# Mixer output projection in two halves with the row factor at the addition, and new borders between stages

## The chip, the cores and the metric

One core of one Trainium2 chip runs the kernel. The metric is the device time of one execution in microseconds (us), the median over several runs. Engines are called PE (TensorE), DVE (VectorE), ACT (ScalarE), POOL (GpSimd) and SP (SyncE, which issues the DMAs). SBUF is the on-chip memory, PSUM the accumulation memory of eight banks that PE writes.

## What is computed

256 tokens of width 1024 go through three layers. Layer 0 is causal attention (16 heads of 64) with q, k rotated and normalized, gated by silu(z), then an output product and a gated addition ("PLE": `x + sigmoid(norm(x) @ w_gate) * (p @ w_proj)`). Layer 1 is a three-branch attention with the same frame. Layer 2 is a mixer (half recurrent, half chunk attention), an attention over 256 memory rows, and an expert layer. The mixer's end is what the title speaks of:

```python
y = concat([rmsnorm(lru_half, norm_grp_a), rmsnorm(attended_half, norm_grp_b)])
x = x + y @ w_out            # rmsnorm(v, g) = v * rsqrt(mean(v * v) + eps) * g, per token
x = x + memory_attention(rmsnorm(x, norm_cross), rmsnorm(mem, norm_mem), ...)
```

A row factor of `rmsnorm` is one number per token, so it can be applied after the product with `w_out`; the gain `g` is per channel and can't.

## The kernel before, in words

**Products in three parts.** All dense products are done in a split form: each fp32 matrix is a high part (`whi`, `hThi`, type fp32r) and a remainder (`wlo`, `hTlo`). A product is the sum of `whi*hThi`, `wlo*hThi` and `whi*hTlo`. Weights come in 88 units of 1 MB (128 x 2048), two units (halves) per chunk of 512 columns. A unit takes 48 matmuls of 256 columns: 16 for each of the three parts. SP loads units into a ring of four slots (L542). ACT writes `whi` (`split`, L1251), of which there are two, so the split of unit u waits for PE's end of unit u-2. POOL writes `wlo = slot - whi` (L1183). PE waits on `hi_ready` and `lo_ready`.

**Activations.** The input of a product is x, transposed on PE by a product with the identity into PSUM, as four "pieces" of 256 channels (`piece`, L641), and then split by ACT or DVE (`piece_hi_act` L1287, `piece_hi_dve` L1782, `piece_lo_dve` L1793). Both wait until PE has ended the last unit that reads the old activations:

```python
def piece_hi_act(name, u):
    act.wait_ge(piece_done, pieces_before(name) + u + 1)
    act.wait_ge(proj_done, units_before(name))
```

The first unit with new activations is `unit_of_pieces` (L663): high parts of pieces 0 and 1, the transposes of the last piece (`last_piece`), high parts of pieces 2 and 3, then all of `wlo`, then the low parts. Chunks in `UNITWISE` go by tokens (`unit_by_tokens`, L691), the others through `project` (L733, L736). The very first activations, `norm0`, have a path of their own: transposes of x (L632), a product with the gain (L1712), a cast (L1716), and remainders on POOL and DVE (L1721). It starts once x, `keep` (the identity) and all of `sml` (gains, tables, p transposed) have landed.

**Row factors.** ACT sums squares (`squares`, L1236), DVE computes mean plus eps (`rsqrt`, L1667), ACT takes the root (L1230), DVE takes the reciprocal and one Newton step (L1669 to L1673), each waiting for the one before. `row_scale` copies the result for ACT (L1694, L1695). All these small operands lie in SBUF (`sc8`). `inverse_root` (L1725 to L1732) does the like for q and k in `rope_chunk`. The constants of the recurrence (`lam`, L1978 on) are computed after the first `row_scale`, in a ping-pong of DVE and ACT (L1367, L1369).

**The stages in question.** After the mixer's inputs (`mix_in`, five chunks), the row scales of the recurrent half go through `rsqrt`, `diagonals` on ACT (L1433) and `row_of_scales` on PE (L953). Then PE waits until ACT has taken v out of PSUM (L1276), and `attention(2)` runs 16 jobs (8 heads x 2 token tiles), software-pipelined: PE scores (L836), DVE maximum (L1876), ACT exponential (L1357), PE transpose (L843), ACT copy (L1348), PE product with v (L854), DVE normalization per group of four jobs (L1887). Then `by_halves` (L994) does the first chunk of `w_out`. Its first half of channels comes from the recurrence (`hThi[:, 0:4]`), its second from the attention, which must first be normalized (`row_norm`, L1685), transposed (`heads`, L1001), multiplied with the gain (L2149) and split (L2153), one token tile after the other. Both weight units are held until the end. A second chunk follows, with the memory rows' pieces transposed in its middle (`memory`). Then come the chunks `mem_k`, `mem_v`, `mem_q`, `attention(3)` (8 jobs), `mem_o` (L663 on), four query chunks, and from about 770 us on the expert layer, which is not touched. The order on every engine is written out by hand.

## Time and profile before

| | us |
|---|---|
| median of 3 runs (lowest to highest) | 1599.39 (1599.07 to 1599.74) |
| the profiled execution, its own time | 1597.65 |
| its span, first to last instruction | 1595.8 |
| PE busy, of the span | 1522.0 |
| DVE, ACT, POOL busy | 897.4, 829.7, 541.1 |
| granted TensorE clock, mean | 0.989 |

PE is busy in 95% of the span, so what matters is where it is not, and what it waited for there. Outside of the start and the end, its idle time comes in many stretches of 0.3 to 4.3 us, between 119 and 732 us. The row "PEclk" of the page gives the granted clock in 40 slices; it is below full in only a few.

### The profile page before, as it was taken

How to read it: one execution, taken by the hardware profiler on the slowest of the kernel's cores; microseconds unless marked ns; L12 is line 12 of the kernel's file. 1: busy time of each engine (PE TensorE's matmuls, PEld its weight loads, DVE VectorE, ACT ScalarE, POOL GpSimd, SP SyncE). 2: the span in 40 equal slices, each digit the busy share in tenths (PEclk: the TensorE clock that was granted, in tenths of full speed). 3: DMA queues.
4: the chain of work that ended last, by engine and by line, in shares of the span. 5: the costliest groups of instructions: out<-in, count | busy, mean ns of one | idle time of the engine just before them, and what ended most of it. 6: DMA issues, size and time to landing. Idle time of an engine off the chain costs nothing.

```text
span 1595.8 us, 27986 instructions
## 1 busy us (share of the span) xinstructions
PE 1522.0 (95%) x10651; PEld 1405.9 (88%) x10651; DVE 897.4 (56%) x2088; ACT 829.7 (52%) x1502; POOL 541.1 (34%) x188
## 2 busy tenths in 40 slices
PE   5999999999999889898999999999999999999998
PEld 5998899978889789888999889999999999999886
DVE  6835348478345532132896995555555555555555
ACT  4546444478355544444455994444444444444444
POOL 5771656510356537726588980000000000000000
PEclk9999999999999899999999999999999999999999
DMA  6741334510134414434254015555555555555553
GB/s 262 285 162 52 127 137 159 211 54 2 55 131 149 168 59 165 148 110 147 80 197 155 1 53 186 186 184 185 184 187 185 188 185 187 186 187 186 173 188 131
DMA packets 37532, 238.51 MB, mean 149 GB/s; under 512 B 4160, under 2 KB 4288, under 8 KB 13248
## 3 DMA queue, kind: packets, MB, share of 16 engines
q1 hardware_dynamic: 37440, 237.27, 42.2%
q8 instruction: 59, 0.97, 0.2%
q14 instruction: 33, 0.27, 0.1%
HBM read 236.21 MB, written 1.05 MB: 149 GB/s over the span
## 4 chain that ended last, share of the span: by engine, by line
PE 67%; ACT 4%; DVE 3%; POOL 3%; issue 2%; ACTq 0%; DVEq 0%
PE bank L1128 22%; PE bank L648 15%; PE bank L651 8%; PE bank L733 5%; PE bank L736 3%; POOL wlo L1183 3%; PE bank L836 3%; PE bank L854 2%; PE bank L691 2%; PE bank L1108 2%; PE bank L663 2%; ACT whi L1251 1%; PE bank L843 1%; PE bank L641 1%; ACT arena L1561 1%
## 5 line engine op out<-in xcount | busy, mean ns | idle before, releaser
L1183 POOL TENSOR_TENSOR wlo<-raw,whi 128x2048 fp32r<-128x2048 f32 x42 | 193.8, 4615 | 199.9 <-ACT whi L1251 199.9
L1183 POOL TENSOR_TENSOR wlo<-arena,whi 128x2048 fp32r<-128x2048 f32 x42 | 194.6, 4638 | 182.9 <-ACT whi L1251 182.9
L648 PE MATMUL bank<-hThi,whi 128*128 128x256 f32 x1024 | 250.3, 282 | 0.0
L648 PE MATMUL bank<-hTlo,whi 128*128 128x256 f32 x1024 | 250.1, 282 | 0.0
L1128 PE MATMUL bank<-whi,ghi 128*128 128x512 f32 x512 | 203.1, 397 | 0.5 <-DVE glo L2307 0.5
L1128 PE MATMUL bank<-whi,glo 128*128 128x512 f32 x512 | 202.9, 396 | 0.0
L1128 PE MATMUL bank<-wlo,ghi 128*128 128x512 f32 x512 | 202.1, 395 | 0.0
L648 PEld LDWEIGHTS bank<-hTlo,whi 128*128 128x128 f32 x1024 | 195.0, 190 | 4.2 <-issue 0.2
L648 PEld LDWEIGHTS bank<-hThi,whi 128*128 128x128 f32 x1024 | 194.7, 190 | 4.2 <-issue 0.2
L1587 ACT ACTIVATE gact<-bank 128x256 f32<-128x256 f32 x96 | 37.1, 386 | 260.5 <-PE bank L651 260.5
L2302 DVE TENSOR_TENSOR gact<-gact,arena 128x256 f32<-128x256 f32 x96 | 40.8, 425 | 189.8 <-ACT gact L1587 189.8
L651 PE MATMUL bank<-hThi,wlo 128*128 128x256 f32 x1024 | 143.7, 283 | 0.0
L1251 ACT ACTIVATE whi<-raw 128x2048 fp32r<-128x2048 f32 x42 | 80.4, 1915 | 105.3 <-PE bank L736 60.4
L651 PEld LDWEIGHTS bank<-hThi,wlo 128*128 128x128 f32 x1024 | 132.1, 192 | 0.0
L1251 ACT ACTIVATE whi<-arena 128x2048 fp32r<-128x2048 f32 x42 | 80.4, 1914 | 99.4 <-PE bank L736 46.2
L2297 DVE TENSOR_TENSOR wlo<-raw,whi 128x1024 fp32r<-128x1024 f32 x84 | 102.9, 1225 | 36.8 <-ACT whi L1591 36.8
L1128 PEld LDWEIGHTS bank<-whi,glo 128*128 128x128 f32 x512 | 96.6, 189 | 23.2
L1128 PEld LDWEIGHTS bank<-whi,ghi 128*128 128x128 f32 x512 | 96.6, 189 | 20.3 <-DVE wlo L2297 1.5
L1128 PEld LDWEIGHTS bank<-wlo,ghi 128*128 128x128 f32 x512 | 96.7, 189 | 19.4
L736 PE MATMUL bank<-whi,hThi 128*128 128x256 f32 x672 | 90.1, 287 | 5.2 <-DVE hThi L1716 5.0
L836 PE MATMUL bank<-arena 128*128 128x256 f32 (+1 forms) x320 | 87.2, 365 | 6.2 <-ACT arena L1276 5.3
L736 PE MATMUL bank<-wlo,hThi 128*128 128x256 f32 x672 | 87.7, 283 | 2.6 <-POOL wlo L1183 2.5
(338 smaller groups left out, 3159.3 us busy)
## 6 DMA issues: line engine op xcount, KB each, us to landing
raw<-ex_in SPq DMA_DIRECT2D x64, 1024.0 KB, 4.7
raw<-w_in SPq DMA_DIRECT2D x44, 1024.0 KB, 4.8
arena<-w_in SPq DMA_DIRECT2D x44, 1024.0 KB, 4.7
xw<-ex_in SPq DMA_DIRECT2D x32, 1024.0 KB, 4.7
raw<-ex_in SPq DMA_DIRECT2D x54, 512.0 KB, 4.1
xw<-ex_in SPq DMA_DIRECT2D x10, 512.0 KB, 4.3
arena<-frt_in SPq DMA_DIRECT2D x1, 3904.0 KB, 15.0
arena<-tab_in SPq DMA_DIRECT2D x1, 1089.0 KB, 16.6
```

The lines of the kernel that those rows point to most:

```text
L648: mm(out, lhs, rhs, start=(k == 0), stop=False)
L651: last = mm(out, lhs, rhs, start=False, stop=(k == len(lo_pairs) - 1))
L663: last = mm(bank[2 * (c % 2) + j][:, 0:UC], lhs, rhs, start=first and k == 0, stop=final and k == KT - 1)
L733: last = mm(bank[2 * (c % 2) + b][:, T * at:T * at + T], w[:, k, P * j:P * j + P], h[:, k, :], start=first, stop=final)
L736: last = mm(bank[2 * (c % 2) + j][:, UC * half:UC * half + UC], h[:, k, P * j:P * j + P], w[:, k, :], start=first, stop=final)
L836: last = mm(score_bank(phase, i)[:, 0:j["nk"]], j["q"][k], j["k"][k], start=(k == 0), stop=(k == len(j["q"]) - 1))
L1128: last = mm(bank[2 * t + h][:, :], g[:, j % 2, tok], w[:, b, at], start=False, stop=(final and i == 2), skip_group_check=True)
L1183: G.tensor_tensor(wlo[:, u % 2, :], slots[u % RING], whi[:, u % 2, :], ALU.subtract).then_inc(lo_ready, 1)
L1251: A(whi[:, u % 2, :], slots[u % RING], ACT.Copy).then_inc(hi_ready, 1)
L1587: A(gact[:, i % 2, :], bank[4 + i % 2][:, 0:T], ACT.Gelu_apprx_tanh).then_inc(a_gelu, 1)
L2297: V.tensor_tensor(wlo[:, b, at], xslots[ex_slot(i)][:, D:2 * D], whi[:, b, at], ALU.subtract).then_inc(vlo_ready, 1)
L2302: V.tensor_tensor(gact[:, i % 2, :], gact[:, i % 2, :], weights, ALU.mult).then_inc(g_ready, 1)
```

## The change

In the parts that matter:

1. **Mixer output.** `by_halves` becomes `by_parts`: unit by unit, each token tile's two halves of channels go to two halves of a bank. The attended half is transposed without its row factor, the first token tile inside `attention(2)` (`heads(0)`), the second after the first 12 matmuls of the projection. `add_parts` adds the first half, then the second times `x_scale`. The second chunk goes the same way.
2. **First rows.** `norm0` becomes pieces like the others. SP issues `keep`, x in two token tiles, the 72 columns of gains, the four weight units, and only then the rest of `sml`. The first two units take `wlo` last. The `lam` constants are computed between the rope chunks.
3. **Borders.** High parts of new activations wait for `hThi_free`, which PE signals after its last read of `hThi`, not at the unit's end. `unit_of_pieces` does three pieces (two for `mem_o`) with their `wlo` before `last_piece`. `unit_by_tokens` takes `wlo` last in its first half. In `take_ple` piece 1 comes before the last tanh.
4. **Small operands in PSUM.** `rsqrt` and `inverse_root` keep theirs in unused columns of a bank.
5. **Around the attentions.** PE's wait for ACT's take of v moves to job 4. One split moves from the last take of `mem_q` into `attention(3)`, and the exponential's table is loaded before it.

```diff
@@ first loads
-            sp_.dma_start(x, x_d).then_inc(x_loaded, 16)
-            sp_.dma_start(keep[:, :], keep_d).then_inc(tab_loaded, 16)
-            sp_.dma_start(sml, sml_d).then_inc(tab_loaded, 16)
+            sp_.dma_start(keep[:, :], keep_d).then_inc(keep_loaded, 16)
+            for t in range(TT):
+                sp_.dma_start(x[:, t], x_d[:, t]).then_inc(x_loaded[t], 16)
+            sp_.dma_start(sml[:, 0:n_gains], sml_d[:, 0:n_gains]).then_inc(gains_loaded, 16)
...
             for u in range(RING):
                 load(u)
+            sp_.dma_start(sml[:, n_gains:NSML], sml_d[:, n_gains:NSML]).then_inc(sml_loaded, 16)
@@ unit_of_pieces
-                for u in range(4):
-                    pe.wait_ge(piece_hi[u], nth(name))
-                    pair(wh, hThi, (2 * u, 2 * u + 1), first=True)
-                    if u == 1 and last_piece is not None:
+                early = 2 if name == "mem_o" else 4 if last_piece is None else 3
...
+                for us in (range(early), range(early, 4)):
+                    if us and us[0] > 0:
                         last_piece()
-                pe.wait_ge(lo_ready, split_before(2 * c) + 1)
-                pair(wl, hThi, range(KT))
+                    for u in us:
+                        pe.wait_ge(piece_hi[u], nth(name))
+                        pair(wh, hThi, (2 * u, 2 * u + 1), first=True)
+                    if c > 0 and us:
+                        pe.wait_ge(lo_ready, split_before(2 * c) + 1)
+                        pair(wl, hThi, range(2 * us[0], 2 * us[-1] + 2))
@@ unit_by_tokens
-                pe.wait_ge(lo_ready, split_before(u) + 1)
...
+                    parts = ((wh, hThi), (wl, hThi), (wh, hTlo)) if half == 1 else ((wh, hThi), (wh, hTlo), (wl, hThi))
+                    for i, (w, h) in enumerate(parts):
+                        if w is wl and j == 0:
+                            pe.wait_ge(lo_ready, split_before(u) + 1)
...
+                        if u in LAST_READS and (i, j) == (1, 1):
+                            last.then_inc(hThi_free, 1)
@@ piece_hi_act (piece_hi_dve alike)
-                act.wait_ge(proj_done, units_before(name))
+                if units_before(name) > 0:
+                    act.wait_ge(hThi_free, frees_before(name))
@@ attention(2) and (3)
+                    if phase == 2 and i == 4:
+                        pe.wait_ge(takenA, taken_before(first_of("mix_out"), "A"))
+                    if phase == 2 and i == 14:
+                        pe.wait_ge(yn_ready, 1)
+                        pe.wait_ge(o_taken, PHASES[2][7]["number"] + 1)
+                        heads(0)
...
-                    if phase == 2 and i == 5:
+                    if (phase, i) in ((2, 5), (3, 1)):
                         split()
@@ the projection on PE
+            def by_parts(i, between):
+                c = first_of("mix_out") + i
+                for half in range(2):
...
+                    late = (i, half) == (1, 0)
+                    def part(j, side):
+                        parts = ((wh, hThi), (wh, hTlo), (wl, hThi)) if late else ((wh, hThi), (wl, hThi), (wh, hTlo))
...
+                    if (i, half) == (0, 0):
+                        part(0, 0)
+                        pe.wait_ge(o_taken, PHASES[2][-1]["number"] + 1)
+                        heads(1)
+                        part(1, 0)
+                        part(0, 1)
+                        pe.wait_ge(half_lo, 2)
+                        part(1, 1).then_inc(proj_done, 1)
+                        continue
@@ rsqrt
-                V.tensor_scalar(var[:, 0:n], of[:, 0:n], inv, EPS, ALU.mult, ALU.add).then_inc(var_ready, 1)
+                v, z = small(count[1], n)
+                y = tmp[:, 0:n]
+                V.tensor_scalar(v, of[:, 0:n], inv, EPS, ALU.mult, ALU.add).then_inc(var_ready, 1)
                 dve.wait_ge(root_ready, count[1])
-                step(V.reciprocal(rinv[:, 0:n], root[:, 0:n]))
-                step(V.tensor_tensor(tmp[:, 0:n], rinv[:, 0:n], rinv[:, 0:n], ALU.mult))
...
+                step(V.reciprocal(y, root[:, 0:n]))
+                step(V.tensor_tensor(z, v, y, ALU.mult))
...
@@ after attention(2) on DVE
-            attended = OR[:, :, CW:D]
-            row_norm(attended, attended, 512, 1, half_rows)
...
+            heads_hi(1)
+            heads_lo(1)
+            squared[0] += 1
+            dve.wait_ge(ss_ready, squared[0])
+            dve.wait_ge(half_lo, 2)
+            y, z = rsqrt(2, 1.0 / 512)
+            step(V.tensor_tensor(x_scale, z, y, ALU.mult))
             row_norm(MEM, MEM, D, 1, piece_rows)
+            add_parts(0, 0)
+            add_parts(0, 1)
+            add_parts(1, 0)
             piece_hi_dve("mem", 1)
             piece_hi_dve("mem", 3)
-            add_chunk(c + 1, 1)
             rest_of_pieces("mem")
+            add_parts(1, 1)
```

PE's instructions at the first chunk of `w_out` before, from the last low part of the recurrent half on (L1001 are the transposes of the attended half, `keep` holds the identity):

```order
L994 MATMUL bank<-whi,hTlo 128x256 x4
L1001 MATMUL bank<-keep,arena 128x128 [waits half_rows]
L1001 MATMUL bank<-keep,arena 128x128 x3
L994 MATMUL bank<-whi,hThi 128x256 [waits half_lo,half_hi]
L994 MATMUL bank<-whi,hThi 128x256 x3
L994 MATMUL bank<-wlo,hThi 128x256 x4
L994 MATMUL bank<-whi,hTlo 128x256 x4
L1001 MATMUL bank<-keep,arena 128x128 [waits half_rows]
L1001 MATMUL bank<-keep,arena 128x128 x3
L994 MATMUL bank<-whi,hThi 128x256 [waits half_lo,half_hi]
```

And now, from the projection's first matmul on (L837 are the transposes, those of the first token tile being already behind):

```order
L1030 MATMUL bank<-whi,hTlo 128x256 x4
L837 MATMUL bank<-keep,arena 128x128 [waits o_taken]
L837 MATMUL bank<-keep,arena 128x128 x3
L1030 MATMUL bank<-whi,hThi 128x256 x4
L1030 MATMUL bank<-wlo,hThi 128x256 x4
L1030 MATMUL bank<-whi,hTlo 128x256 x4
L1030 MATMUL bank<-whi,hThi 128x256 x4
L1030 MATMUL bank<-wlo,hThi 128x256 x4
L1030 MATMUL bank<-whi,hTlo 128x256 x4
L1030 MATMUL bank<-whi,hThi 128x256 [waits half_lo]
```

Where two round trips to DVE stood directly behind the transposes, 24 matmuls now stand between the only transposes left and the wait for them.

ACT's first instructions before (L1236 are the sums of squares, L1251 the splits of weights, L1367 and L1369 the steps of `lam`):

```order
L1236 ACTIVATE arena,sc<-xw 128x1024 [waits x_loaded]
L1236 ACTIVATE arena,sc<-xw 128x1024 [waits achain]
L1251 ACTIVATE whi<-raw 128x2048 [waits w_loaded0]
L1251 ACTIVATE whi<-raw 128x2048 [waits w_loaded1]
L1230 ACT_TABLE_LOAD
L1230 ACTIVATE sc<-sc 128x2 [waits var_ready]
L1367 ACT_TABLE_LOAD
L1367 ACTIVATE arena<-arena 128x4 [waits lam_v]
L1369 ACT_TABLE_LOAD
L1369 ACTIVATE arena<-arena 128x4 [waits lam_v]
L1251 ACTIVATE whi<-arena 128x2048 [waits proj_done,w_loaded2,scale_ready]
```

And now (L1388 and L1395 are the sums of squares, L1312 the high parts of pieces, L1275 the splits):

```order
L1388 ACTIVATE arena,sc<-xw 128x1024 [waits x_loaded0]
L1312 ACTIVATE hThi<-bank,arena 128x256 [waits piece_done,gains_loaded,achain]
L1312 ACTIVATE hThi<-bank,arena 128x256
L1312 ACTIVATE hThi<-bank,arena 128x256 [waits piece_done]
L1312 ACTIVATE hThi<-bank,arena 128x256
L1275 ACTIVATE whi<-raw 128x2048 [waits w_loaded0]
L1275 ACTIVATE whi<-raw 128x2048 [waits w_loaded1]
L1395 ACTIVATE arena,sc<-xw 128x1024 [waits x_loaded1]
L1254 ACT_TABLE_LOAD
L1254 ACTIVATE sc<-bank 128x2 [waits var_ready]
L1275 ACTIVATE whi<-arena 128x2048 [waits proj_done,w_loaded2,scale_ready]
```

The two steps of `lam` no longer stand ahead of the third split, and two pieces of the activations stand ahead of the first.

## Rows read from the trace of the kernel before

**Rows 1.** The page: busy time, share and instructions of each engine.
```profile
PE 1522.0 (95%) x10651; PEld 1405.9 (88%) x10651; DVE 897.4 (56%) x2088; ACT 829.7 (52%) x1502; POOL 541.1 (34%) x188
```

**Rows 2.** Who PE waited for, whole span: us in total, times, longest us.
```profile
PE bank L733 <- POOL wlo L1183: 5.3, 7, 2.0
...
PE bank L663 <- ACT hThi L1287: 4.3, 4, 1.1
...
PE bank L691 <- POOL wlo L1183: 3.2, 3, 1.1
```

**Rows 3.** Timeline, 0 to 60 us: start, duration, engine, operation, count [idle <-releaser].
```profile
8.72 4.10 PE L632 MATMUL bank<-keep,xw 128*128 128x128 f32 x16 [8.72 <-DVEq L1974]
...
11.04 1.91 ACT L1251 ACTIVATE whi<-raw 128x2048 fp32r<-128x2048 f32 x1 [2.93 <-DMA raw<-w_in]
...
13.03 4.50 POOL L1183 TENSOR_TENSOR wlo<-raw,whi 128x2048 fp32r<-128x2048 f32 x1 [12.58 <-ACT whi L1251]
...
13.52 1.91 ACT L1251 ACTIVATE whi<-raw 128x2048 fp32r<-128x2048 f32 x1 [0.57 <-DMA raw<-w_in]
13.75 4.07 DVE L1716 CAST hThi<-arena 128x512 fp32r<-128x512 f32 x1
...
17.88 3.42 PE L736 MATMUL bank<-whi,hThi 128*128 128x256 f32 x16 [5.05 <-DVE hThi L1716]
...
21.14 2.08 PE L736 MATMUL bank<-wlo,hThi 128*128 128x256 f32 x16
...
35.73 2.18 PE L736 MATMUL bank<-wlo,hThi 128*128 128x256 f32 x16 [2.48 <-POOL wlo L1183]
...
39.67 2.08 PE L736 MATMUL bank<-whi,hThi 128*128 128x256 f32 x16
```

**Rows 4.** DMA issues, 0 to 60 us: median us to landing.
```profile
arena<-sml_in SPq DMA_DIRECT2D x1, 772.0 KB, 6.9
```

**Rows 5.** Timeline, 150 to 223 us: first unit of the first PLE gate.
```profile
180.61 1.19 PE L663 MATMUL bank<-whi,hThi 128*128 128x256 f32 x8 [1.08 <-ACT hThi L1287]
...
187.42 2.08 PE L736 MATMUL bank<-whi,hThi 128*128 128x256 f32 x16
```

**Rows 6.** Timeline, 466 to 514 us: row scale of the mixer input, and what waits.
```profile
477.67 2.48 DVE L1667 TENSOR_SCALAR sc<-sc 128x2 f32<-128x2 f32 x1 [0.17 <-ACT arena L1236]
...
482.28 1.90 ACT L1251 ACTIVATE whi<-raw 128x2048 fp32r<-128x2048 f32 x1
...
488.88 1.22 PE L733 MATMUL bank<-hThi,wlo 128*128 128x256 f32 x8 [1.98 <-POOL wlo L1183]
```

**Rows 7.** Timeline, 514 to 558 us: start of the mixer's attention.
```profile
535.97 4.37 DVE L1670 TENSOR_TENSOR sc<-sc 128x2 f32<-128x2 f32 x1
...
540.37 0.16 DVE L1671 TENSOR_TENSOR sc<-sc 128x2 f32<-128x2 f32 x1
...
541.86 0.68 PE L953 MATMUL bank<-arena 128*128 128x128 f32 x4 [0.70 <-ACT arena L1433]
...
545.30 0.40 ACT L1357 ACTIVATE arena<-arena,sc 128x128 f32<-128x128 f32 x1 [0.91 <-DVE sc L1876]
```

**Rows 8.** Windows: stretch, length, busy of PE, PEld, DVE, ACT, POOL; clock, DMA share, GB/s.
```profile
546.00:556.00 10.00, 8.82 (x33) 7.05 (x33) 4.54 (x21) 7.91 (x27) 4.53 (x1) 0.52 0.09 16
```

**Rows 9.** Timeline, 557 to 620 us: the mixer's output projection.
```profile
564.83 0.72 PE L994 MATMUL bank<-whi,hThi 128*128 128x256 f32 x4
...
573.31 0.89 PE L994 MATMUL bank<-whi,hThi 128*128 128x256 f32 x4 [2.04 <-DVE hTlo L2153]
...
583.19 2.08 PE L736 MATMUL bank<-whi,hThi 128*128 128x256 f32 x16
...
598.02 2.15 PE L663 MATMUL bank<-hThi,whi 128*128 128x256 f32 x16 [1.08 <-ACT hThi L1287]
```

**Rows 10.** Timeline, 637 to 682 us: start of the memory attention.
```profile
675.97 5.41 PE L836 MATMUL bank<-arena 128*128 128x256 f32 x16 [2.54 <-ACT arena L1276]
...
678.49 0.51 ACT L1357 ACTIVATE arena<-arena,sc 128x256 f32<-128x256 f32 x1 [1.26 <-DVE sc L1876]
```

305 lines of the change are left out of this document (165 added, 140 removed).

## The prediction

> **What bounds the kernel now.** I read the page first, then the waits of PE, then the timeline at each place that the change touches. The page shows PE busy for 1522.0 of 1595.8 us [rows 1], so at most 74 us can be won, and only where PE stands idle or runs at a lower clock. The waits [rows 2] name the releasers: ACT's high parts L1287 at the first unit after a change of activations (four waits, 4.3 in all), POOL's `wlo` in `unit_by_tokens` (three, 3.2) and in `project` (seven, 5.3). The rest lies at the start, where the first matmul begins at 17.88 [rows 3], and around the mixer's attention [rows 7 to 9]. From 770 us on nothing is changed and the time only shifts.
>
> **The unit of account.** A group of 16 matmuls costs 1.92: its record says 2.08, but records overlap by 0.16 (17.88 + 3.42 is 0.16 past the next start, 21.14) [rows 3]. A weight unit is three groups, 5.76. ACT's split takes 1.91, POOL's `wlo` 4.50 [rows 3].
>
> **1. Start: 9.9 (7.5 to 10.5).** The first 17.88 us hold three things in sequence: x, `keep` and 772 KB of `sml` landing 6.9 after issue [rows 4], 4.10 of transposes from 8.72, and casts on DVE. The last cast takes 4.07, exactly beside POOL's first `wlo` [rows 3]. Now only 36 KB of gains go ahead of the weights, so 736 KB fewer. Two weight units of 1024 KB let ACT's splits begin 2.48 apart (11.04 and 13.52) [rows 3], so 736 KB are worth 1.8: first split at 9.2, first weights high at 11.15, first `wlo` at 15.7. The activations come earlier and no cast stands beside POOL. First matmul at 11.2. The first group is slow again (3.26 from start to start), the low parts follow to 16.4, then `wlo`: the first unit ends at 18.3, the second at 24.05. The third split must wait for the end of the first unit: 18.3 + 1.91 + 4.6 makes its `wlo` ready at 24.8, while PE wants it at 26.0. So the wait of 2.48 at 35.73 goes too, since no step of `lam` stands ahead of that split any more. The fourth unit starts at 29.8 instead of 39.67. The low end keeps the 2.4.
>
> **2. `unit_by_tokens`, `wlo` last in the first half: 3.2 (1.6 to 3.2).** Three waits of 1.07 [rows 2]; in that half 16 matmuls of low parts (1.92) come before `wlo` is needed, more than each wait. What is late next is the following split, which the low end pays.
>
> **3. First units with three pieces ahead: 1.15 (-0.5 to 2.2).** The high parts may start when PE has made its last read of `hThi`, one group of eight (0.96) before the unit's end, so most of the 1.08 in front of the first matmul goes [rows 5]. In exchange the last piece's transposes stand later, with one pair behind them: the way through DVE, which took 2.04 with low parts [rows 9], is without them about 1.0 and mostly bare, of which I take 0.5 as new. Net 0.55 for each of two PLE units, 0.25 and 0.2 for two others, 0.2 for `mem_o`, and -0.6 for the layer 1 output, where more stands bare. The low end is all six with the 1.0 bare and half of the gain.
>
> **4. Row scale of the mixer input: 1.8 (0.7 to 2.5).** DVE's operation on 2 elements at 477.67 takes 2.48, until POOL's `wlo` is over; the same kind takes 0.16 elsewhere [rows 6, 7]. The split at 482.28 stands behind it, and PE waits 1.98 at 488.88 for its `wlo`. With the operand in PSUM, 2.3 of ACT's delay go and the wait ends in part on the next link. The Trainium skill ("SBUF — State Buffer", "Who interferes with whom") says that DVE and GpSimd share a port pair which the one that holds it keeps for a whole instruction. The trace agrees (2.48 and 4.37 where 0.16 is usual). By that page the steps of `lam`, which stay in SBUF and now stand between the rope chunks, can each be blocked as well.
>
> **5. Start of the mixer's attention: 3.95 (2.4 to 5.4).** The same block costs 4.37 at 535.97 where 0.16 stands at 540.37 [rows 7]. ACT's diagonals, PE's four matmuls at 541.86 and the take of v follow it, and the first exponential comes at 545.30. Unblocked, the scale is ready 4.2 earlier, before PE ends `mix_in` at 541.16; ACT takes v at once, and PE's scores no longer wait for it. First exponential 542.45: 2.85. From 546 to 556 the granted clock is 0.52, so PE is nearly all the time at 1.2 GHz, after this idle; PE is busy 8.82 of 10 there and ACT 7.91 [rows 8]. At 2.4 GHz ACT would bound it, so at most 2.1 come back; I take 1.5, and 0.4 off for the first tile's transposes inside.
>
> **6. Mixer output: 5.8 (3.5 to 7).** Before, from 564.83 to the ready end of the second chunk, 598.02 - 1.08 = 596.94, are 32.1 [rows 9]. The new order needs four units (23.04), four transposes (0.48) and the memory's 16 (1.67): 25.2. The two waits of 2.04 and the slow matmuls behind the first (0.89 for four, elsewhere 0.72 or less) go, since 24 matmuls (2.9) stand ahead of the wait for the second tile, whose way through DVE took 2.04. New is a wait in the second chunk: its first split needs PE to be done with the first unit and ACT to be through its roots and squares, which I estimate at 7.2 after the attention's end from the durations of these operations, so with 1.9 and 4.6 `wlo` stands at 13.8 where PE wants it at 12.65: 1.2. That gives 26.4, a gain of 5.7, and 0.1 at the memory's pieces: their high parts start earlier, but DVE's additions come in front.
>
> **7. Cross border: 1.4 (0.5 to 1.6).** One more wait of 1.08 by the same row [rows 2], whole here since `hThi_free` comes 1.92 before the end, and 0.3 of waits for `wlo` behind it.
>
> **8. Memory attention: 2.0 (0 to 3).** PE waits 2.54 for ACT's take, behind a split of 1.91; the first exponential is at 678.49 [rows 10]. Without the split ahead it comes about 3 earlier, and 1 is given back where the split now stands between two jobs.
>
> **9. `lam` between the rope chunks: -0.5 (-3.6 to 0).** The steps have all operands in SBUF, and one caught beside POOL may last 4.4 [rows 7]. ACT waits for them within its takes. PE has a unit's cover, so I take little; the low end is one block of 4.4 with 0.8 hidden.
>
> The sum is 28.7 (all low ends 12.1, all high ends 35.4). The profiled execution has 1597.65, so 1569.0; the median is 1.74 above it: **1570.7**.
>
> **The rivals.** **A, the chain hands the waits back (0.15).** Nothing speeds up ACT or POOL; each split waits for PE's end two units before, and POOL adds 4.5. Where a wait for `wlo` goes, the next unit may meet the chain one step later, as the seven waits in `project` show [rows 2]. Against it: a split and a `wlo` are 6.4 against two units of 11.5, so a delay dies out within a unit if ACT is free. It would cost term 2 whole (3.2), 1.0 of term 4, 0.5 of term 7 and 3.6 of terms 6 and 8: 20.4 are left, 1579.
>
> **C, at the mixer output the change doesn't do what it says (0.10).** DVE has the last group's normalization, the first tile's split and both parts of the second tile in sequence; if PE's last part waits there as before, 4.5 of term 6 are lost: 1575.2.
>
> **B, slower (0.03).** TensorE stays at its lower level after the new start. The first matmuls run at half speed before: 3.26 for the first group, 1.92 for the second [rows 3]. The new start has transposes, idle, and one group after another with waits for low parts and `wlo`. Each unit at 1.2 GHz adds 5.76; the gain of 28.7 and the 3.2 that count as no change are gone after 5.5 units, and the time is over 1602.6. Against it: PE did rise within one group before, after 5.05 of idle. The Trainium skill ("TensorE: Matmul & The Clock Gate", "What's actually happening") says that the slow level is the default and activity lifts it; the trace agrees, and 10 us at 0.52 in the attention show that broken work can keep it low [rows 8].
>
> **How the numbers follow.** My forecast has 0.70, A 0.15, C 0.10, B 0.03, and 0.02 are for smaller losses that together leave no change. A measurement of this kernel can tell 0.2%, 3.2 us, from no change. Faster is then 0.95, same 0.02, slower 0.03. The range: independent errors of the terms (the largest 2.4 on terms 1 and 6) give some 5 to either side, 1564 to 1576; case A and its mixtures reach to 1583.
>
> **What would show it.** In the new profile: first matmul near 11, fourth unit near 29.8; no wait of L691's kind; every operation of `rsqrt` at 0.16 to 0.2; the first exponential of the mixer's attention 2.9 sooner after `mix_in`, and a granted clock near 1 there; no wait of 2.04 in the output, one of about 1.2 in its second chunk; about 1.0 of idle behind the last piece. Wrong would be: waits for `wlo` in the units after those named, DVE late with the second tile, or a low clock over whole units behind 11 us.

## The result and the profile after

| | before | changed |
|---|---|---|
| median of 4 executions, us | 1599.23 | 1570.53 |
| lowest to highest | 1597.09 to 1599.74 | 1569.33 to 1571.22 |
| profiled execution, its own time | 1597.65 | 1571.22 |
| its span | 1595.8 | 1569.4 |

The ratio is 0.9825, 95% interval 0.9813 to 0.9838. The forecast was 1570.7, so the time is right. The two profiled executions lie 26.4 apart, though, not 28.7: the sum of the terms was taken from the own time of the profiled one (1597.65 to 1569.0), and against that pair it was some 2.2 too high. That the medians agree to 0.2 is in part luck. Which terms held is read from the traces. One execution of a kernel below (u3, 1970.65) had a granted clock of 0.69 over its whole span and is left out of that kernel's median.

The page of the changed kernel, its busy times; they answer to [rows 1]:

```profile
PE 1513.6 (96%) x10651; PEld 1401.3 (89%) x10651; DVE 872.7 (56%) x2097; ACT 830.7 (53%) x1507; POOL 538.0 (34%) x186
```

Who PE waited for in the changed kernel (us in total, times, longest us), against [rows 2]:

```profile
PE bank L749 <- POOL wlo L1206: 4.6, 6, 1.7
PE bank L650 <- DVE arena L2260: 4.3, 1, 4.3
PE bank L673 <- DVE hThi L1813: 3.9, 5, 0.8
PE bank L673 <- DVE hThi L1811: 3.1, 3, 1.6
PE bank L673 <- ACT whi L1275: 2.7, 1, 2.7
...
PE bank L673 <- ACT hThi L1312: 1.6, 3, 0.6
...
PE bank L1030 <- POOL wlo L1206: 1.1, 1, 1.1
```

The three waits of `unit_by_tokens` are gone. The wait of 4.3 before the last border, for the scaled rows, was there before. The waits for ACT's high parts have gone from 4.3 to 1.6, and in their place stand waits for the last piece's high parts from DVE: 3.9 and 3.1, of which one of 1.57 is the last heads' in `mem_o`, as before.

The timeline of the changed kernel, 0 to 60 us (start, duration, engine, operation, count, idle and releaser), against [rows 3]:

```profile
5.53 3.64 PE L650 MATMUL bank<-keep,xw 128*128 128x128 f32 x16 [5.53 <-DMA xw<-x_in]
...
9.88 1.93 ACT L1275 ACTIVATE whi<-raw 128x2048 fp32r<-128x2048 f32 x1
...
11.86 3.78 PE L673 MATMUL bank<-whi,hThi 128*128 128x256 f32 x16 [2.69 <-ACT whi L1275]
11.89 9.13 POOL L1206 TENSOR_TENSOR wlo<-raw,whi 128x2048 fp32r<-128x2048 f32 x2 [11.43 <-ACT whi L1275]
...
15.45 3.09 PE L673 MATMUL bank<-whi,hTlo 128*128 128x256 f32 x16
...
18.37 2.08 PE L673 MATMUL bank<-wlo,hThi 128*128 128x256 f32 x16
...
31.81 2.08 PE L752 MATMUL bank<-whi,hThi 128*128 128x256 f32 x16
...
51.74 4.27 DVE L2065 TENSOR_TENSOR arena<-arena,sc 128x4 f32<-128x4 f32 x1
```

From the first start to the second are 3.59, to the third 2.92: both groups are slow, and the fourth unit starts at 31.81 where it started at 39.67. No wait is left inside. The last row is a step of `lam`, held up beside a `wlo` of POOL (51.35 to 55.98) as term 9 feared, 4.27 long; PE's groups went on 1.92 apart behind it, so it cost nothing.

The mixer's attention in the changed kernel, 512 to 546 us, against [rows 7]:

```profile
521.49 0.17 DVE L1707 TENSOR_TENSOR bank<-bank,sc 128x2 f32<-128x2 f32 x1
...
527.69 0.40 ACT L1383 ACTIVATE arena<-arena,sc 128x128 f32<-128x128 f32 x1
...
530.37 1.89 ACT L1275 ACTIVATE whi<-raw 128x2048 fp32r<-128x2048 f32 x1
...
532.48 0.43 PE L878 MATMUL bank<-arena 128*128 128x64 f32 x2 [1.94 <-ACT arena L1374]
```

And the windows there (stretch, length, busy of PE, PEld, DVE, ACT, POOL, granted clock, DMA share, GB/s), against [rows 8]:

```profile
530.00:535.00 5.00, 2.40 (x14) 1.83 (x14) 1.14 (x8) 4.84 (x13) 2.66 (x1) 0.82 0.02 5
535.00:540.00 5.00, 5.00 (x18) 3.94 (x17) 2.59 (x9) 2.61 (x9) 1.87 (x1) 0.50 0.39 138
```

The operation on two elements takes 0.17 where it took 4.37, and the first exponential comes at once. But from 535 to 540 PE is at 1.2 GHz, busy all of the time: the lower clock has come back, behind the 1.94 in which PE waited while ACT did a split.

The output projection of the changed kernel, 540 to 600 us, against [rows 9]:

```profile
548.02 0.72 PE L1030 MATMUL bank<-whi,hThi 128*128 128x256 f32 x4
...
562.27 0.74 PE L1030 MATMUL bank<-wlo,hThi 128*128 128x256 f32 x4 [1.11 <-POOL wlo L1206]
...
590.26 1.22 PE L749 MATMUL bank<-hThi,wlo 128*128 128x256 f32 x8 [1.66 <-POOL wlo L1206]
```

Neither wait of 2.04 is left, and one of 1.11 for `wlo` has come: forecast was 1.2. The wait at 590.26, behind the first unit on the memory rows, was 1.14 before (at 612.34) and is now 0.52 longer.

### The profile page after: what moved, and what is told of

The parts are those of the page before. It is cut to its first block, busy times and chain, and to the rows that moved or that the text cites. A ratio compares the mean times of both kernels' runs of the same rounds, so it can differ in the third digit from the quotient of the medians.

```text
span 1569.4 us, 28028 instructions
## 1 busy us (share of the span) xinstructions
PE 1513.6 (96%) x10651; PEld 1401.3 (89%) x10651; DVE 872.7 (56%) x2097; ACT 830.7 (53%) x1507; POOL 538.0 (34%) x186
## 4 chain that ended last, share of the span: by engine, by line
PE 52%; ACT 2%; issue 1%; DVE 1%; POOL 1%; DMA 0%; ACTq 0%; DVEq 0%
PE bank L1158 22%; PE bank L658 15%; PE bank L661 8%; PE bank L749 2%; PE bank L1138 2%; PE bank L673 1%; ACT arena L1595 1%; POOL wlo L1206 1%; ACT xw L1598 1%; PE bank L1097 0%; PE bank L752 0%; PE bank L709 0%; DMA raw<-ex_in 0%; DVE wlo L2367 0%; ACT raw L1605 0%
## 5 line engine op out<-in xcount | busy, mean ns | idle before, releaser
L1275 ACT ACTIVATE whi<-arena 128x2048 fp32r<-128x2048 f32 x42 | 80.4, 1915 | 102.9 <-PE bank L752 47.7
L1275 ACT ACTIVATE whi<-raw 128x2048 fp32r<-128x2048 f32 x42 | 80.4, 1914 | 94.1 <-PE bank L752 52.9
L1625 ACT ACTIVATE whi<-raw 128x1024 fp32r<-128x1024 f32 x84 | 88.4, 1053 | 2.1 <-DMA raw<-ex_in 2.1
L860 PE MATMUL bank<-arena 128*128 128x256 f32 (+1 forms) x320 | 84.0, 354 | 2.4 <-ACT arena L1300 1.6
L1940 DVE CUSTOM_DVE_ANT_0 arena<-bank,arena 128x256 f32<-128x256 f32 (+1 forms) x152 | 51.9, 344 | 61.8 <-PE bank L860 42.8
```

What stands on the lines that cost most here:

```text
L860: last = mm(score_bank(phase, i)[:, 0:j["nk"]], j["q"][k], j["k"][k], start=(k == 0), stop=(k == len(j["q"]) - 1))
L1275: A(whi[:, u % 2, :], slots[u % RING], ACT.Copy).then_inc(hi_ready, 1)
L1625: A(whi[:, b, at], xslots[ex_slot(i)][:, D:2 * D], ACT.Copy).then_inc(vhi_ready, 1)
L1940: V.tensor_tensor_reduce(out=Msb[n % 3][:, 0:j["nk"]], in0=score_bank(phase, i)[:, 0:j["nk"]], in1=j["mask"], scale=-j["scale"], scalar=1e ...
```

## Where the time came from, term by term

ACT's 84 splits come in the same order in both kernels, so the difference of their starts tells how far the changed one is ahead. It stands still within the long runs of units, and steps at the borders. In us:

| place (terms of the sum) | ahead behind it | step | forecast |
|---|---|---|---|
| start (1) | 7.86 | 7.9 | 9.9 |
| first eight chunks, layer 0 attention (9) | 7.8 | 0.0 | -0.5 |
| first PLE, one `unit_by_tokens` (2, 3) | 10.0 | 2.1 | 2.1 |
| layer 1 attention and first output unit (3) | 11.6 | 1.6 | -0.6 |
| second PLE, one `unit_by_tokens` (2, 3) | 13.3 | 1.8 | 1.6 |
| mixer input (4) | 14.7 | 1.3 | 1.8 |
| mixer's attention (5) | 16.8 | 2.15 | 3.95 |
| mixer output (6) | 22.1 | 5.25 | 5.8 |
| cross border (7) | 23.5 | 1.5 | 1.4 |
| memory attention and `mem_o` (8, 3) | 26.5 | 2.95 | 2.2 |
| last `unit_by_tokens` and last border (2) | 26.5 | 0.1 | 1.1 |

(For the mixer's attention the first matmul of the projection is compared, 564.83 and 548.02.) Three terms were too large by 2.0, 1.8 and 1.0, two too small by 2.2 and 0.7. The experiments are about these.

## Experiments: one part undone

Each kernel is the changed one with the edit that is shown, and is compared with the changed one's 1570.53. The groups of experiments ran at other times and on other chips than it. Between the groups the median of the kernel before lay between 1598.2 and 1599.3, so a difference of about one microsecond from 1570.53 tells nothing. One execution of each kernel has a trace. "Split by split" compares the starts of ACT's 84 splits in two traces, as in the table.

All four ran beside the kernel before on the same chip (1598.83, 7 executions).

**The small operands back in SBUF (u1).**

```diff
-            b = bank[small_bank[call - 1]]
-            return [b[:, 464 + 16 * i:464 + 16 * i + n] for i in range(2)]
+            return [var[:, 8 * i:8 * i + n] for i in range(2)]
```

> The changed kernel with one thing undone: the two small operands of rsqrt lie in SBUF again, not in PSUM. My theory (DVE is held up by POOL wherever an operation has all operands in SBUF): an operation of rsqrt that meets a wlo of POOL lasts 2 to 4.4 us again, and the two places lose what they won: about 1.3 at the mixer input (where the trace of the change won that much between the splits), 2.9 at the first exponential of the mixer's attention; together some 4 us, 1574.5, with 0.5 more or less elsewhere. Rival (the earlier first exponential comes from PE's scores no longer waiting for the take): rsqrt may be held up, but the attention starts as in the change, and at most 1.5 are lost, 1572.

Measured: 1575.06, ratio to the kernel before 0.9847 (0.9831 to 0.9864). Its timeline at the start of the mixer's attention:

```profile
524.89 4.37 DVE L1705 TENSOR_TENSOR sc<-sc 128x2 f32<-128x2 f32 x1
...
533.20 0.40 ACT L1382 ACTIVATE arena<-arena,sc 128x128 f32<-128x128 f32 x1
```

and at the mixer input:

```profile
468.33 0.72 DVE L1702 TENSOR_SCALAR sc<-sc 128x2 f32<-128x2 f32 x1
...
477.80 1.21 PE L748 MATMUL bank<-hThi,wlo 128*128 128x256 f32 x8 [1.51 <-POOL wlo L1205]
```

and at the very start, where the first row scale stands beside POOL's first `wlo`:

```profile
17.03 4.08 DVE L1705 TENSOR_TENSOR sc<-sc 128x2 f32<-128x2 f32 x1
```

The block of 4.37 is back to the hundredth, so what lies in SBUF is what POOL holds up. The first exponential stands 5.5 behind its place in the change (527.69), of which 3.6 had been there before this border: 1.9 by the operand, not 2.9. At the mixer input only 0.72 are lost, since the squares come so late now that POOL's `wlo` is nearly over; the next wait for `wlo` is 0.57 longer (0.94 in the change). The total agrees with my 4, but not for my reason. Split by split, 0.8 of the 3.9 behind the last split arise in the first 33 us and 2.2 more between 315 us and the end of the layer 1 output, where this execution had a low clock for longer than the change's (last section). At the start the block of 4.08 makes ACT's third split 1.4 late and brings a wait of 0.32 for `wlo` at 28.66: 0.6 of the 0.8. So the operand itself is worth 0.6 at the start, which I had not counted, 0.6 at the mixer input and 0.4 at the attention's end, 1.6 in this trace (the rest of the 4.5 between the medians it doesn't explain), as the attention hands most of the 1.9 back: after 535 us the changed kernel is at 1.2 GHz, and this one has a granted clock of 1.00 from 530 to 540 and of 0.83 in the ten behind.

**All of `sml` ahead of the weights (u2).**

```diff
+            sp_.dma_start(sml[:, n_gains:NSML], sml_d[:, n_gains:NSML]).then_inc(sml_loaded, 16)
             for u in range(RING):
                 load(u)
-            sp_.dma_start(sml[:, n_gains:NSML], sml_d[:, n_gains:NSML]).then_inc(sml_loaded, 16)
```

> The changed kernel with the remaining 736 KB of sml sent before the four weight units instead of behind them. My theory (the start is bound by what lands before the first weight unit): the first split comes 1.8 later (11.7 instead of 9.88), and all after it the same 1.8, time 1572.3. Rival (the start is bound by PE's lower clock and POOL's first wlo, not by the landing): under 0.8 is lost.

Measured: 1572.82, 0.9833 (0.9817 to 0.985). Its first matmuls and split:

```profile
11.53 1.91 ACT L1275 ACTIVATE whi<-raw 128x2048 fp32r<-128x2048 f32 x1 [1.08 <-DMA raw<-w_in]
13.49 3.78 PE L673 MATMUL bank<-whi,hThi 128*128 128x256 f32 x16 [4.21 <-ACT whi L1275]
...
17.08 2.94 PE L673 MATMUL bank<-whi,hTlo 128*128 128x256 f32 x16
```

The first split is 1.65 later, the third 1.48, and the two slow groups are the same. But this trace alone can't carry the price of 736 KB: in u3, which loads as the change does, the first split is 1.51 later too (11.40). The medians say more: 2.3 above the change and 1.3 above u3, where 1.8 was forecast and the rival allowed under 0.8. So the landing counts for about what I took, as far as the medians tell. The larger part of what term 1 had wrong is in n5.

**The order of the first unit as before (u3).**

```diff
-                early = 2 if name == "mem_o" else 4 if last_piece is None else 3
...
+                for u in range(4):
+                    pe.wait_ge(piece_hi[u], nth(name))
+                    pair(wh, hThi, (2 * u, 2 * u + 1), first=True)
+                    if u == 1 and last_piece is not None:
+                        last_piece()
+                if c > 0:
+                    pe.wait_ge(lo_ready, split_before(2 * c) + 1)
+                    pair(wl, hThi, range(KT))
```

> The changed kernel with unit_of_pieces as it was: the last piece's transposes after the first two pieces, all of wlo behind all high parts. My theory (of each border, the early hThi_free gives 0.96 and the three pieces ahead cost some 0.5 net of the idle before): each of the seven borders with a last piece is about 0.5 to 0.8 faster with the old order, 3 to 5 in sum, 1566 to 1568. Rival (the order is what pays, since high parts of the last pieces would come late without the wlo of the first three as cover): the time is 2 to 4 longer, 1573 to 1575.

Measured: 1571.51 (1569.46 to 1572.04, three executions), 0.9822 (0.9802 to 0.9841). Neither theory: the order makes no difference that the time shows. The waits tell why:

```profile
PE bank L650 <- DVE xw L2020: 2.6, 2, 1.3
PE bank L673 <- DVE hThi L1809: 1.9, 2, 1.6
...
PE bank L673 <- DVE hThi L1811: 1.5, 5, 0.3
```

Of 7.0 for DVE's high parts 3.4 are left, but 2.6 come for the source of the last piece (the PLE's last rows, which DVE has not written when PE asks after two pieces). With three pieces ahead the source is there; it is the transposes' place behind `wlo` that leaves their way through DVE bare. A gain of up to 2 by the old order isn't ruled out, though: this trace ends level with the change's, but 1.1 of it were lost by the later landing at the start and 1.5 in layer 1, where the clock was low for longer, while the borders of the second PLE and of the mixer input were 0.5 and 0.6 shorter.

**The cover of the second token tile taken away (u4).**

```diff
                     if (i, half) == (0, 0):
                         part(0, 0)
+                        part(1, 0)
+                        part(0, 1)
                         pe.wait_ge(o_taken, PHASES[2][-1]["number"] + 1)
                         heads(1)
-                        part(1, 0)
-                        part(0, 1)
                         pe.wait_ge(half_lo, 2)
```

> The changed kernel with the transposes of the second token tile behind the 24 matmuls which now cover them, so that PE goes straight into the wait for the low parts. My theory (the cover is what took the two waits of 2.04 away): one wait of about 1.9 to 2.0 comes back before the last part of the first unit, perhaps with slow matmuls behind it, 1572.4 to 1574. Rival (something else, such as fewer round trips alone, made the gain, and the next wait for wlo hides this one): the wait of 1.1 for wlo in the second chunk shrinks by what is lost here, and under 1.2 remains, 1571.6.

Measured: 1573.99, 0.9843 (0.9827 to 0.986). Its projection:

```profile
554.05 0.74 PE L1030 MATMUL bank<-whi,hThi 128*128 128x256 f32 x4 [2.04 <-DVE hTlo L1883]
...
564.12 0.74 PE L1030 MATMUL bank<-wlo,hThi 128*128 128x256 f32 x4 [1.66 <-POOL wlo L1206]
```

The wait of 2.04 returns to the hundredth, and the wait for `wlo` doesn't shrink but grows by 0.55, as ACT's split is late too. The trace is 2.9 later behind it (from 1.0 ahead to 1.9 behind). The cover is the mechanism of term 6.

## Experiments: something added or moved

These four ran together; the kernel before had 1599.33 (7 executions).

**PE kept busy at the start (n5).**

```diff
             pe.wait_ge(keep_loaded, 16)
+            for i in range(16):
+                nc.tensor.transpose(bank[3][:, 0:P], ident, ident)
             for t in range(TT):
                 pe.wait_ge(x_loaded[t], 16)
                 for u in range(4):
                     piece("norm0", u, (t,))
+            for i in range(32):
+                nc.tensor.transpose(bank[3][:, 0:P], ident, ident)
```

> The changed kernel with 16 more transposes of the identity before those of x and 32 behind them, into a bank that is overwritten later; nothing else differs. In the change the first group took 3.59 and the second 2.92 from start to start, where 1.92 is usual. My theory (PE is at its lower clock there because it had stood idle, and POOL's first wlo at 16.45 is the next bound): with PE kept busy the first two groups take 1.92, the third waits for wlo until 16.45 instead of starting at 18.37, and 1.9 are won, 1568.6. Rival (the two groups are slow for another reason, such as the first reading of hThi and whi, or the clock doesn't rise on such work): no gain, 1570.5, or up to 1 lost where the added transposes delay those of x.

Measured: 1569.78, 0.9818 (0.9801 to 0.9834). Its start:

```profile
7.93 3.66 PE L890 MATMUL bank<-keep 128*128 128x128 f32 x32
11.63 2.17 PE L673 MATMUL bank<-whi,hThi 128*128 128x256 f32 x16
...
13.64 2.08 PE L673 MATMUL bank<-whi,hTlo 128*128 128x256 f32 x16
16.33 2.17 PE L673 MATMUL bank<-wlo,hThi 128*128 128x256 f32 x16 [0.61 <-POOL wlo L1210]
```

Both slow groups are at full pace and the third split is 1.95 earlier, as forecast. But the start of the change isn't the same in each execution. Six other kernels have the very same program there, and their first groups of `wlo` begin at 17.18 (n7), 17.37 (u4), 18.08 (n8), 18.19 (n6), 18.66 (c9) and 19.46 (u3, by its later landing), for 18.37 in the change. In u4:

```profile
11.95 2.68 PE L673 MATMUL bank<-whi,hThi 128*128 128x256 f32 x16 [2.69 <-ACT whi L1275]
```

With the added transposes (n5 and the later c10, c11, c12) they begin at 16.33, 17.37, 16.98 and 16.36. So the added work is worth 1.4 on the average of these starts, and less than nothing to 3.1 from one pair of executions to another. With it both groups ran at full pace in all four executions, without it in none of the seven. The median is only 0.75 lower than that of the change, which can't be told from none; this execution lost 2.5 in the layer 1 attention, at a clock that was low for 10.2 us there and for 3.4 in the change's.

**The split of the mixer's attention at its tenth step (n6).**

```diff
-                    if (phase, i) in ((2, 5), (3, 1)):
+                    if (phase, i) in ((2, 10), (3, 1)):
                         split()
```

> The changed kernel with ACT's split inside the mixer's attention at its tenth step instead of its fifth. In the change PE stands idle for 1.94 while that split (1.89) runs, and the granted clock is 0.52 from 533 to 538. My theory (that idle time brings the lower clock, which then costs 1 to 2): without it the clock stays at 1.0, the attention ends 1.5 to 3 sooner, 1567.5 to 1569. Rival (the split costs ACT its 1.9 wherever it stands, and the clock falls because the attention's small matmuls never keep PE busy enough at the start): the same time within 0.7, the clock falls all the same.

Measured: 1568.52, 0.9807 (0.9791 to 0.9824). The same windows in it:

```profile
530.00:535.00 5.00, 3.79 (x25) 2.95 (x25) 3.18 (x16) 4.68 (x22) 0.00 (x0) 1.00 0.39 159
535.00:540.00 5.00, 3.54 (x24) 2.89 (x23) 3.26 (x12) 4.63 (x13) 1.05 (x1) 1.00 0.00 0
```

The clock stays at 2.4 GHz and ACT is the bound, with 4.6 to 4.7 of 5. The split costs PE 1.47 at its new place, but the clock doesn't fall after it. This doesn't hang on one trace: in all eight executions with the split at the fifth step (the change, u1 to u4, n5, n7, n8) the clock falls 2.0 to 4.8 us after that split's start, and in none of the five with the split at the tenth step (n6 and c9 to c12) does it fall within the attention. From the 41st split to the 59th the execution went from 2.0 behind the change to 1.0 ahead: 3.0 for the attention (the median gives 2.0; the execution shown was itself the slowest of its four, 1571.05, by the 2.0 of the layer 1 attention).

**The last piece's transposes ahead of `wlo` (n7).**

```diff
                 for us in (range(early), range(early, 4)):
-                    if us and us[0] > 0:
-                        last_piece()
                     for u in us:
                         pe.wait_ge(piece_hi[u], nth(name))
                         pair(wh, hThi, (2 * u, 2 * u + 1), first=True)
+                    if us and us[0] == 0 and early < 4:
+                        last_piece()
                     if c > 0 and us:
```

> The changed kernel with the last piece's transposes between the high parts of the first three pieces and their wlo, in all eight borders (two and two pieces in mem_o). In the change PE waits 0.78 after these transposes in each of seven, as 12 matmuls (1.44) stand ahead of them and nothing behind. My theory (these waits are bare and on the path that sets the end, and what the last piece is made of is there 1.5 sooner): seven waits of 0.78 go, 5 to 5.5 us, 1565. Rival (the last piece's source is late, so that PE waits at the transposes instead, or the next wait for wlo takes it): under 2 are won.

Measured: 1565.10, 0.979 (0.9774 to 0.9807), so 5.4 below the change. Its mixer border:

```profile
455.67 0.66 PE L650 MATMUL bank<-keep,xw 128*128 128x128 f32 x4
456.08 1.68 PE L673 MATMUL bank<-hThi,wlo 128*128 128x256 f32 x12
457.60 0.64 PE L673 MATMUL bank<-hThi,whi 128*128 128x256 f32 x4
```

In the change the last row has a wait of 0.79 before it (at 463.00). Here the 12 matmuls of `wlo` fill it, and the source was ready. All seven are gone, and nothing took their place.

**The memory attention's split back in the take (n8).**

```diff
-                    if c in ACROSS and not (j == 1 and c == first_of("mem_o") - 1):
+                    if c in ACROSS:
...
-                    if (phase, i) in ((2, 5), (3, 1)):
+                    if (phase, i) == (2, 5):
```

> The changed kernel with the split of the memory attention back in the last take, ahead of it, as in the kernel before. The change won 2.95 there (split to split), where I had forecast 2.0. My theory (the take of v waits for this split, and the scores for the take): the first exponential comes 1.9 to 2.5 later, the jobs behind it don't stall for the split, and 1 to 2.5 are lost, with a lower clock over part of the scores, 1572 to 1573. Rival (the gain at this border came from the exponential's table being loaded before and from hThi_free): under 0.7 is lost.

Measured: 1573.58, 0.9845 (0.9828 to 0.9862). The scores of its first jobs:

```profile
651.89 5.34 PE L860 MATMUL bank<-arena 128*128 128x256 f32 x16 [2.54 <-ACT arena L1300]
```

This is [rows 10] again, 2.54 of wait and 16 matmuls in 5.34, where the change has 3.72 behind a wait of 0.69. In the trace 2.9 are lost against the change from the cross border to the first split behind the attention. Term 8 was right in kind, and its size lacked the clock: I had counted the take, not that the scores behind an idle PE run at half speed.

## Experiments: do the gains add?

Four more kernels, with one more miss. The kernel before had 1598.22 (9 executions) beside the first three.

**Both splits later, and one split ahead of the memory rows' roots (c9).** To the transposes ahead of `wlo` and the split at step ten come:

```diff
-                if i == 5:
+                if i == (5, 11)[phase]:
                     split()
...
             squares(MEM, D)
+            split()
             roots(2)
-            split_on(first_of("mix_out"))
+            split()
             split()
```

> Built for speed, and to see whether the gains add: the changed kernel with the last piece's transposes ahead of wlo (as in n7), the split of the mixer's attention at its tenth step (as in n6), the split of the layer 1 attention at its eleventh step instead of its fifth, and ACT's next split after the mixer's attention before the roots of the memory rows instead of behind them. My theory (each lies at its own border and nothing takes it back): 5.4 of n7, 2.0 to 2.9 of n6, 1 to 3 in the layer 1 attention (PE idle for 1.52 beside that split, then a clock of 0.8 over some 8 us), 0.6 to 0.9 at the wait of 1.11 for wlo in the output's second chunk: 1558.5 to 1561.5. Rival (the lower clock comes back at other moments, since the attentions keep PE busy only in part): the first and last items stay and the clock stays low for some us in one of the two attentions, 1562 to 1564.

Measured: 1566.94, 0.9804 (0.979 to 0.9817), worse than n7 alone. Its timeline in the output:

```profile
547.82 1.90 ACT L1275 ACTIVATE whi<-arena 128x2048 fp32r<-128x2048 f32 x1
...
550.80 4.79 DVE L1723 TENSOR_SCALAR arena<-arena,sc 128x1024 f32<-128x1024 f32 x2
...
557.22 1.04 PE L1030 MATMUL bank<-whi,hThi 128*128 128x256 f32 x4 [3.92 <-DVE xw L1897]
```

A new wait, by the mechanism of term 5 on a large operation. The earlier split let POOL start its `wlo` at 549.79, DVE's normalization of the memory rows fell beside it and took 4.79 where the change has 1.42, the additions behind it were late, and PE waited 3.92 for its bank and then ran at half speed. Its operands all lie in SBUF. The Trainium skill ("SBUF — State Buffer", "Who interferes with whom") describes such a block for a whole instruction of the holder; the trace agrees (DVE's work of 1.42 ends 1.2 behind POOL's end at 554.38). c12 below, without that earlier split, bears this out: the same operation takes 1.42 and the wait is gone. The later split in the layer 1 attention gave nothing that the traces show: from the 37th split to the 41st this kernel loses 0.3 on the change, and so did n7 without it.

**With the transposes at the start (c10)**, as in n5:

> The one before it with the 48 added transposes at the start (as in n5). My theory: in n5's trace the third split was 1.95 earlier and all behind it kept that until the layer 1 attention; against the kernel before it here 0.7 to 1.9 are won. Rival (a start with a higher clock only moves the moments at which the clock falls later): no difference that can be measured.

Measured: 1566.47, 0.9798 (0.9785 to 0.9811): 0.5 less, which doesn't tell the two theories apart. In its trace 1.2 are won at the third split against c9's, and 1.5 lost at a stretch of low clock from 217 to 220 that no other execution has.

**With 30 transposes ahead of the last border (c11):**

```diff
+            for i in range(30):
+                nc.tensor.transpose(bank[7][:, 0:P], ident, ident)
             for u in range(3):
                 scaled_piece(u)
```

> The one before it with 30 more transposes of the identity in the idle time of 4.27 ahead of the last border (the expert layer's pieces), where PE waits for the scaled rows and then runs its transposes and first matmuls at a clock of 0.5 for some 7 us. My theory (the idle time brings the lower clock): with PE kept busy for 3.6 of the 4.27, the clock stays at 1.0 and the unit's 28 matmuls, 16 transposes and the waits between them take 1.5 to 2.5 less. Rival (the added transposes end late, or the DVE and ACT steps between them bound that stretch): under 0.5 is won, or something is lost.

Measured: 1566.47, the same. The traces show the gain all the same: at this border c11 gains 2.4 on the change and c10 gains 1.2, so 1.3 are by the added work, in this pair. Between two medians of five executions that spread by 2.6 and 3.2 it can't be told.

**The parts that had held (c12).** Transposes ahead of `wlo`, split at step ten, and both sets of added transposes:

> The parts that had held, without the two that had not: the changed kernel with the transposes ahead of wlo (n7), the split of the mixer's attention at its tenth step (n6), the added transposes at the start (n5) and ahead of the last border (c11); the layer 1 split and the split after the mixer's attention are where the change has them. My theory (in c9 the split moved ahead of the memory rows' roots started POOL's wlo sooner, DVE's row_norm of the memory rows fell beside it and took 4.79 instead of 1.42, and PE waited 3.9 for the addition behind it): that wait is gone, the one of 1.11 for wlo is back, and the sum of 5.4 (n7), about 2 (n6), 0.7 (n5) and 1.3 to 2.4 (c11 against c10) off 1570.5 gives 1559.5 to 1562. Rival (the gains of a higher clock don't add, since the clock falls at another moment): 1563 to 1565, no better than n7 alone.

Measured: 1560.83 (1558.94 to 1561.75, 5 executions) beside 1599.24 of the kernel before, 0.9761 (0.9746 to 0.9776). It beats both kernels, the changed one by some 9.7. It lies inside the forecast, and below the rival's 1563. Its windows in the mixer's attention and at the last border:

```profile
530.00:540.00 10.00, 8.45 (x64) 7.29 (x63) 5.94 (x23) 8.93 (x27) 4.54 (x1) 1.00 0.24 78
...
685.00:693.00 8.00, 7.00 (x58) 6.23 (x57) 5.09 (x14) 4.84 (x12) 4.27 (x2) 1.00 0.43 142
```

For comparison, the changed kernel at its last border:

```profile
695.00:703.00 8.00, 3.95 (x19) 3.95 (x20) 5.02 (x14) 5.53 (x12) 4.27 (x2) 0.62 0.38 132
```

With PE busy through the wait the clock is 1.00 where it was 0.62.

## Why the prediction was right, and where its terms were not

**Term 1, 9.9 forecast, 7.9 measured.** The step that failed is "the first group is slow again (3.26 from start to start), the low parts follow to 16.4". The second group was slow as well (3.59 and 2.92), with PE idle for 2.69 behind its transposes. The sum should have had 2.9 for the low parts, and `wlo` then starts at 18.37 in place of 16.4. Of these 2.0, 1.0 are the second group, 0.3 the first, and 0.7 the landing (first split at 9.88 for 9.2). n5, c10, c11 and c12 show that it was the idle PE: kept busy, it ran both groups at full pace. The size is this execution's; in u4 and n7 the same program lost 1.0 and 1.2 less.

**Terms 2 and 3** held where the clock was not in play: 2.1 for 2.1 and 1.8 for 1.6. The step on the layer 1 output (-0.6) came out at 1.6, and the order isn't why. Half of it, 0.8, was won in the attention ahead of the unit (the kernel before is 10.07 behind at its matmuls at 327.62 and 317.55, and 10.86 behind at those at 350.02 and 339.16). There its clock was low for 6.8 us and the changed one's for 3.4. The other 0.7 came in the output unit, where the kernel before had a low clock and the changed one had not, and the last piece's 0.78 stands bare as forecast. As the same program shows either clock (last section), neither can be put down to the change; of the -0.6 itself only the bare 0.78 can be seen. The windows of the kernel before and of the changed one at that unit:

```profile
409.00:413.00 4.00, 3.48 (x18) 3.34 (x17) 1.84 (x4) 0.00 (x0) 0.00 (x0) 0.60 0.00 0
```

```profile
397.00:401.00 4.00, 3.40 (x28) 3.12 (x27) 2.00 (x7) 0.38 (x1) 0.00 (x0) 1.00 0.00 0
```

**Term 4, 1.8 and 1.3.** The wait of 1.98 is now 0.94. Half of it is by the operand in PSUM (0.57, u1). The rest I put down to the squares' new time, which u1 keeps; no run takes that away alone.

**Term 5, 3.95 and 2.15.** The first exponential was right: 2.95 for 2.85. What failed is "I take 1.5" for the clock. ACT's split at the fifth step, which I hadn't named, makes PE idle for 1.94 and the clock still falls, if for 6.8 us in place of 10.2. n6 takes that split away from there and the clock stays up.

**Term 6, 5.8 and 5.25.** Both waits of 2.04 gone, 1.11 come for 1.2. u4 shows the cover as the cause. Up to the first matmul on the memory rows (598.02 before, 575.43 now) 5.8 were won, just the forecast. One unit later 0.5 were handed back, by the wait for `wlo` at 590.26.

**Terms 7 and 8.** 1.5 for 1.4. For the memory attention 2.95 with `mem_o`, for 2.2, by the clock (n8).

**The last border, 0.1 for 1.1.** I had counted only the wait for `wlo` taken away. It did win 1.3 (26.5 ahead became 27.8), and 1.2 were handed back at the border behind it. The late last piece waits 0.79 where 0.31 stood before, so 0.5 are by the order. The rest goes with the clock: behind the same idle time of 4.27 it was low for 6.8 us in this execution and for 3.4 in that of the kernel before; in n5, with 3.4, the border took 0.6 less. c11, with PE busy through the wait, has no low clock there.

**The rivals.** A (waits handed back one unit later) came only once and small, with the 0.5 at 590.26 where it asked for 8.3 in all: along the runs of units the lead stood still to 0.1, and what was handed back at the last border has another cause. C didn't come. B, PE staying at its lower level, happened for one group more than forecast in the change's trace, not for units. The rule that the Trainium skill gives ("TensorE: Matmul & The Clock Gate", "What's actually happening"), that the slow level is the default and activity lifts it, agrees with n5 and c11, where added work alone brought the clock up or kept it there.

## What to carry to other kernels

Count a wait of PE twice: by its own length, and by what runs at half speed behind it. In this kernel the second part came to some 1.3 to 2 us each at the start, in the mixer's attention and at the last border, and useless transposes in the idle time, or a split moved out of an attention's first steps, gave it back: together with the transposes ahead of `wlo` 9.7 us (c12), though of the single steps only n6's and n7's show in the medians. A round trip through DVE needs work of the same unit placed behind its start, not ahead of it (12 matmuls moved behind four transposes took away seven waits of 0.78 and gave 5.4 us), and before an operation of ACT is moved forward, look at which DVE operations on SBUF the POOL operation that it releases will now stand beside.

## What was not expected of the hardware

The lower clock is not the same from one execution to the next, and that isn't the program. The change, u4, n6 and n8 are the same program up to 530 us, their ACT starts its third split within 1.0 us of each other, and three of them within 0.3. In the layer 1 attention, from 315 to 329 us, they have these windows (the change, n8, n6; u4 has 0.88 as the change):

```profile
315.00:329.00 14.00, 11.92 (x75) 10.13 (x73) 11.57 (x46) 11.04 (x42) 4.52 (x1) 0.88 0.22 76
```

```profile
315.00:329.00 14.00, 10.29 (x75) 8.70 (x75) 11.62 (x46) 11.04 (x42) 4.51 (x1) 1.00 0.21 76
```

```profile
315.00:329.00 14.00, 12.40 (x60) 11.17 (x61) 9.80 (x36) 9.43 (x34) 4.52 (x1) 0.63 0.21 76
```

So the clock was low there for 3.4 us, not at all, and for 10.2 us. The first two have the same 75 matmuls; n6 has 60 and came out 2.2 us later, as did n5 with 2.5. At the layer 1 output (some 400 us) it was low in the kernel before, u1, u3 and c11, and in none of the others.

This is as large as most terms here. It also goes with the spread of the medians' executions: of the nine of the kernel before that ran beside c12, the fastest (1594.99) has a mean granted clock of 0.994 and the slowest (1601.00) one of 0.986, with the others in between in nearly the same order. A difference of 2 us between two single traces is therefore not a gain until the granted clock of both has been compared over that stretch. What decides in which execution the clock falls stays open.
